# Inverting the chunk matrices of a gated delta-rule scan by 16 by 16 halves, with the joins in the scan's last rounds

## The reference, cut to what matters

```python
tmat = eye + beta[:, None] * (k @ k.T) * dec_strict          # unit lower triangular, per chunk
wk, uv = triangular_solve(tmat, [beta * gam * k, beta * v])
a_qk = (q @ k.T) * dec_incl
def step(s, ...):
    u = uv - wk @ s
    o = gam * (q @ s) + a_qk @ u
    s = g_end * s + k_dec.T @ u
```

## Time and profile before

| | |
|---|---|
| median of 3 runs | 3227.69 us (3227.17 to 3240.73) |
| the profiled execution | 3231.66 us, span 3229.6 us, mean granted TensorE clock 0.917 |
| PE busy | 2796.0 us (87% of the span) |
| DVE, ACT, POOL busy | 1320.1, 1064.8 and 1286.7 us |
| phase of the heads | from about 190 to 1245 us |

### The profile page before, as it was taken

The page is one execution under the profiler, slowest core; times in us unless marked ns, Lnnn a source line. Parts: engine busy times, 40 slices in busy tenths (PEclk is TensorE's granted clock), DMA queues, the critical chain, the costliest instruction groups (busy, mean ns, idle before and its releaser), DMA issues. The chain is left out here.

```text
span 3229.6 us, 45798 instructions
## 1 busy us (share of the span) xinstructions
PE 2796.0 (87%) x17857; PEld 1766.7 (55%) x18113; DVE 1320.1 (41%) x1836; ACT 1064.8 (33%) x1794; POOL 1286.7 (40%) x1450
## 2 busy tenths in 40 slices
PE   5666878878887878989998978999899999999996
PEld 2234656656665665567676754455455555555554
DVE  5233555545555544666767655351311111110112
ACT  4123343443443443244454535211512111101122
POOL 1036747657467450276666531242212111211121
PEclk8777988988889878999999999999999999999997
DMA  7511121112111113223334336241011111111111
GB/s 278 179 57 52 33 74 56 45 59 71 39 66 64 39 52 108 90 67 83 87 85 132 81 91 223 76 165 46 25 41 39 46 39 39 39 46 39 37 35 65
DMA packets 244520, 241.22 MB, mean 75 GB/s; under 512 B 26285, under 2 KB 216286, under 8 KB 241014
## 3 DMA queue, kind: packets, MB, share of 16 engines
q1 hardware_dynamic: 231238, 207.32, 20.9%
q10 hardware_dynamic: 11520, 21.01, 1.7%
q0 software_dynamic: 1584, 10.49, 0.8%
HBM read 191.12 MB, written 43.45 MB: 73 GB/s over the span
## 5 line engine op out<-in xcount | busy, mean ns | idle before, releaser
L171 POOL TENSOR_TENSOR w_pair<-w_raw,w_pair 128x1024 bf16<-128x1024 f32 (+1 forms) x156 | 367.6, 2357 | 1226.7 <-ACT w_pair L166 1225.0
L182 PE MATMUL t_out<-hn,w_pair 128*128 128x512 bf16 (+1 forms) x3102 | 572.2, 345 | 17.1 <-DVE hn L2759 10.5
L1043 PE MATMUL bank<-hn,w_pair 128*128 128x512 bf16 (+1 forms) x2251 | 476.2, 364 | 41.9 <-POOL w_pair L171 22.1
L182 PEld LDWEIGHTS t_out<-hn,w_pair 128*128 128x128 bf16 x3168 | 310.5, 98 | 278.5 <-issue 18.3
L182 PE MATMUL t_out<-ys,w_pair 128*128 128x512 bf16 (+1 forms) x2118 | 397.6, 347 | 10.6 <-PEq L2400 8.4
L1043 PEld LDWEIGHTS bank<-hn,w_pair 128*128 128x128 bf16 x2304 | 239.1, 104 | 227.5 <-issue 50.6
L2095 PE MATMUL s_banks<-hn,w_pair 128*128 128x512 bf16 (+1 forms) x1677 | 315.1, 344 | 7.5 <-PEq L1656 4.9
L182 PEld LDWEIGHTS t_out<-ys,w_pair 128*128 128x128 bf16 x2160 | 213.4, 99 | 190.1 <-issue 16.8
L166 ACT ACTIVATE w_pair<-w_raw 128x1024 bf16<-128x1024 f32 x156 | 164.1, 1054 | 440.4 <-PE t_out L182 321.3
L182 PE MATMUL b_out<-ys,w_pair 128*128 128x512 bf16 (+1 forms) x1129 | 216.6, 353 | 40.6 <-DVE ys L2495 29.5
L2095 PEld LDWEIGHTS s_banks<-hn,w_pair 128*128 128x128 bf16 x1728 | 169.3, 98 | 142.5 <-POOL w_pair L171 5.2
(11 more groups left out here) (402 smaller groups left out, 4412.9 us busy)
## 6 DMA issues: line engine op xcount, KB each, us to landing
w_raw<-in_w_in SPq DMA_DIRECT2D x56, 512.0 KB, 4.0
w_ada_rows<-in_w_ada SPq DMA_DIRECT2D x24, 1024.0 KB, 5.3
w_raw<-in_w_gu SPq DMA_DIRECT2D x44, 512.0 KB, 3.8
hn<-scratch_g SPq DMA_DIRECT2D x24, 640.0 KB, 5.7
scratch_g<-gate_ring ACTq DMA_DIRECT2D x48, 256.0 KB, 2.3
mat<-scratch_cum SPq DMA_DIRECT2D x16, 640.0 KB, 4.7
at<-scratch_cum SPq DMA_DIRECT2D x16, 640.0 KB, 5.7
qg<-scratch_cum SPq DMA_DIRECT2D x16, 640.0 KB, 7.7
```

The costliest lines, as they stand in the source:

```text
L171: pool.tensor_tensor(K.w_pair[:, slot, 1, 0:kt, :], K.w_raw[:, slot, 0:kt, :], K.w_pair[:, slot, 0, 0:kt, :], ALU.subtract).then_inc(K.w_l ...
L182: mm = pe.matmul(out[:, c0:c0 + cn], K.w_pair[:, slot, w, k, :], x[:, a, k, c0:c0 + cn], start=i < 3, stop=i >= 9 * kt - 3)
L1043: mm = pe.matmul(bank[:, 6 + n % 2, 0:cn], K.w_pair[:, slot, w, k, :], K.hn[:, a, k, c0:c0 + cn], start=i == 0, stop=i == 23)
```

## The change

- POOL inverts the 16 by 16 diagonal halves of the 32 by 32 blocks, both at once: 15 steps of a multiply and a subtract, each on 2 times (15 - j) times (j + 1) elements. One more memset clears half of `mat_d`.
- What joins two halves to a block of 32 becomes three parts of 80 matmuls on 32 by 32 tiles of the array, with 16 columns (`join16`). Part W stands in round 6 (rounds count from 0) after its first piece of projection, part Z at the end of round 6, part X after round 7. ACT copies W out (`read_w16`), DVE adds Z and X into `zd` and `ld`.
- DVE's two turns of the inverse move from the tail into round 5 of the scan (places 10 and 11); the adds stand at places 15 and 17.
- The tail is written in another order on PE, DVE, ACT and POOL, and the Q tile comes in nine pieces. The turned values are scaled by DVE (six `tensor_tensor`) and no longer by ACT (twenty `activation`). POOL prepares `mat` before the low half of the V tile. The low half of the Q tile follows that of Z after step 14.

```diff
-                    for j in range(31):
-                        a, b = 31 - j, j + 1
-                        tmp = step[:, 0:a * b].rearrange("p (i c) -> p i c", c=b)
+                    for j in range(15):
+                        a, b = 15 - j, j + 1
+                        tmp = step[:, 0:2 * a * b].rearrange("p (s i c) -> p s i c", s=2, c=b)
                         pool.drain()
-                        pool.tensor_tensor(tmp, mat_in[:, j, j + 1:32].unsqueeze(2).to_broadcast([P, a, b]),
-                                           x[:, j:j + 1, 0:b].to_broadcast([P, a, b]), ALU.mult)
+                        pool.tensor_tensor(tmp, m16[:, :, j, j + 1:16].unsqueeze(3).to_broadcast([P, 2, a, b]),
+                                           x16[:, :, j:j + 1, 0:b].to_broadcast([P, 2, a, b]), ALU.mult)
                         pool.drain()
-                        i = pool.tensor_tensor(x[:, j + 1:32, 0:b], x[:, j + 1:32, 0:b], tmp, ALU.subtract)
+                        i = pool.tensor_tensor(x16[:, :, j + 1:16, 0:b], x16[:, :, j + 1:16, 0:b], tmp, ALU.subtract)
...
+                    if is_head(m):
+                        decays_mat(m)
                     if is_head(n + 1):
                         low(("V", n + 1))
                     if is_head(m):
-                        decays_mat(m)
                         inverse(m, {2: [t for t in (("K", m + 1),) if is_head(t[1])],
-                                    14: [t for t in (("Z", n + 1),) if is_head(t[1])],
-                                    26: [t for t in (("Q", n + 2),) if is_head(t[1])]})
+                                    14: [t for t in (("Z", n + 1), ("Q", n + 2)) if is_head(t[1])]})
...
+                def join16(n, part):
+                    b = bank[:, 2, 0:2 * NB * 16].rearrange("p (i c) -> p i c", c=16)
+                    if part == "W":
+                        pe.wait_ge(s.diag16, 2 * n + 1)
+                    elif part == "Z":
+                        pe.wait_ge(s.diag16, 2 * n + 2)
+                        pe.wait_ge(s.w16, n + 1)
+                    else:
+                        pe.wait_ge(s.z16, n + 1)
+                    for i in range(2 * NB):
+                        d, t = divmod(i, NB)
+                        for q in range(4):
+                            p = slice(32 * q, 32 * q + 32)
+                            if part == "W":
+                                mm = pe.matmul(b[p, i, :], mat[p, d, t, p], zd[p, i, 16:32], start=True, stop=True)
+                            elif part == "Z":
+                                mm = pe.matmul(b[p, i, :], ld[p, i, :], mat_d[p, i, 16:32], start=True, stop=True)
+                            else:
+                                mm = pe.matmul(b[p, i, :], mat_d[p, i, :], ld[p, i, 0:16], start=True, stop=True)
+                    mm.then_inc(s.join16, 1)
...
+                    def join16(place):
+                        if place == 10:
+                            dve.wait_ge(s.inv, n + 1)
+                            dve.transpose(zd[:, :, :].rearrange("p b i -> p i b"), x).then_inc(s.diag16, 1)
+                        if place == 11:
+                            dve.transpose(ld[:, :, :].rearrange("p b c -> p c b"), x.rearrange("p i c -> p c i")).then_inc(s.diag16, 1)
+                        if place == 15:
+                            dve.wait_ge(s.join16, 3 * n + 2)
+                            dve.tensor_tensor(zd[:, 0:2 * NB, 16:32], zd[:, 0:2 * NB, 16:32], b16, ALU.add).then_inc(s.z16, 1)
+                        if place == 17:
+                            dve.wait_ge(s.join16, 3 * n + 3)
+                            dve.tensor_tensor(ld[:, 0:2 * NB, 0:16], ld[:, 0:2 * NB, 0:16], b16, ALU.add)
+                            dve.drain().then_inc(s.diag_out, 1)
...
+                def read_w16(n):
+                    act.wait_ge(s.join16, 3 * n + 1)
+                    act.activation(mat_d[:, 0:2 * NB, 16:32], bank[:, 2, 0:2 * NB * 16].rearrange("p (i c) -> p i c", c=16),
+                                   ACT.Copy, scale=half[:, :]).then_inc(s.w16, 1)
...
+                        for g, (t0, tn) in enumerate(GROUPS):
+                            b = quad(to_read(h, f"VT{g}"), tn)
+                            dve.tensor_tensor(vt[:, 0, t0:t0 + tn, :], b, per_tok(skb[:, t0:t0 + tn], tn), ALU.mult)
+                            dve.tensor_tensor(vt[:, 1, t0:t0 + tn, :], b, per_tok(sk[:, t0:t0 + tn], tn), ALU.mult)
+                            dve.drain().then_inc(s.read_dve, 1)
```

More of the change, by code:

```diff
@@ L794, in read_by_act @@
 def read_by_act(name):
-    return name in ("VT0", "VT1", "VT2") or name[:3] in ("L1V", "L1E", "L2V", "L2F") and name[3] == "1"
+    return name[:3] in ("L1V", "L1E", "L2V", "L2F") and name[3] == "1"
 USES = bank_uses()
@@ L814, in phase_heads @@
         mat = f("mat", 2, NB, C)
-        mat_d, mat_in = f("mat_d", 32, 32), f("mat_in", 32, 32)
+        mat_d, mat_in = f("mat_d", 32, 32), f("mat_in", 33 * 32)
+        half = f("half_col", 1)
         x_step = f("inv_x", 32 * 32 + 256)
@@ L831, in phase_heads @@
         bp, nbg = f("beta_n", 2, 2, NB), f("neg_bg", 2, NB)
-        rk2, sk, skb = f("k_inv2", NB), f("k_len", NB), f("k_len_b", NB)
+        rk2, sk, skb = (mat_in[:, 32 * 32 + 10 * j:32 * 32 + 10 * j + NB] for j in range(3))
         kss, eq = f("k_sum", 2, NB), f("q_eps", 2, NB)
@@ L1189, in _, with piece @@
                     after = [("Q", n + 1)] if is_head(n + 1) else []
-                    def piece(c):
+                    def piece(first, end):
                         if after:
-                            fill(after, 24 * c, 24)
+                            fill(after, first, end - first)
+                    if h == -1:
+                        for last in [x for x in USES if x[0] < h][-3:]:
+                            pe.wait_ge(s.read_act if read_by_act(last[1]) else s.read_dve, READ_NUMBER[last])
+                        for part in "WZX":
+                            join16(n, part)
+                    piece(0, 8)
                     if is_head(n):
-                        for g in range(3):
-                            turned(h, f"KT{g}", lambda t: blk(kt[:, n % 3], t))
                         pe.wait_ge(s.diag_out, n + 1)
@@ L1219, in _ @@
                         sums(h, "SSK", lambda t: rw[:, 2 + off(t):2 + off(t) + C])
+                    piece(14, 20)
+                    if is_head(n):
+                        pe.wait_ge(s.y_diag, 2 * n + 1)
+                        for d in range(2):
+                            for half in range(2):
+                                level2_v(h, d, half)
+                        pe.wait_ge(s.silu, SILU["V", n] + 1)
+                        for g in range(3):
+                            turned(h, f"VT{g}", lambda t: blk(vt_raw, t))
+                    piece(20, 36)
                     if h >= 0:
@@ L1233, in _ @@
                             products(h, f"G{g}", kt[:, m % 3], kt[:, m % 3])
+                    piece(52, 62)
+                    if is_head(n):
+                        for g in range(3):
+                            products(h, f"QK{g}", kt[:, n % 3], qt)
+                    piece(62, 72)
             @block.scalar
@@ L1401, in _ @@
                     if is_head(n):
-                        level2(h, 0)
-                        for d in range(2):
-                            act.wait_ge(s.qg_in[d], 16 * (n + 1))
-                            act.activation(qg[:, d, :], qg[:, d, :], ACT.Exp).then_inc(s.qg_exp, 1)
                         for d in range(2):
@@ L1408, in _ @@
                             act.activation(at[:, d], at[:, d], ACT.Exp).then_inc(s.at_exp, 1)
+                    if is_head(m):
+                        for d in range(2):
+                            act.wait_ge(s.mat_clamp, 2 * m + d + 1)
+                            act.activation(mat[:, d], mat[:, d], ACT.Exp).then_inc(s.mat_exp, 1)
+                    if is_head(n):
+                        level2(h, 1)
                     if h >= 0:
@@ L1418, in _ @@
                     if is_head(m):
-                        for d in range(2):
-                            act.wait_ge(s.mat_clamp, 2 * m + d + 1)
-                            act.activation(mat[:, d], mat[:, d], ACT.Exp).then_inc(s.mat_exp, 1)
                         act.wait_ge(s.mat, m + 1)
@@ L1461, in tap @@
                             conv_tap(t, w)
+                        if h >= 0 and is_head(n):
+                            join16(place)
                     for i, units in enumerate(ROUNDS if h >= 0 else ()):
```

181 lines of the change are left out of this document (100 added, 81 removed).

## The result

The changed kernel takes **3248.02 us** (median of 20 runs, 3234.84 to 3255.18); the kernel before took 3230.86 us beside it (20 runs). The ratio is 1.0048, interval 1.0037 to 1.0058: a little slower, where 2% faster was forecast. The profiled execution took 3241.40 us (span 3239.6).

A forecast was written before the change was run, and what follows sets the result against it. Scans were taken as bound by PE's own work, tails by some 22.5 us of waits and the clock. Six turns (-47), the front (-5) and the last tail (-7.5) gave -60 us: 3168 us, range 3145 to 3190.

The forecast's parts named there:

- The inverse: On POOL, it ends 25 us into the scan; DVE asks about 38 us in; cost nothing, 13 us to spare.
- The joins: On PE, 1.85 us for each part of 160 records; W and Z add 3.7 us to the scan, X lies in the tail.
- Start of the tail: From the scan's last output product to `level1_v`: 4.8 us instead of 13.1, the idle 10.9 us gone.
- Middle and end of the tail: PE's work becomes 45 us, ACT's copy starts at 38; the next scan starts at about 53 instead of 65.65 us.
- Start of the scan: The output's low half comes last on DVE ahead of the first `rhs`: 1 us more.
- The sum: Per turn: tail -12.6, joins +3.7, scan's start +1, together -7.9 us; six turns -47, all -60 us.
- At the front: Ahead of the first scan PE's idle 23.39 us becomes 16.5; with scan 0 and the rest of that tail about -5 us.
- at the end: In the last tail, waits of 6.67 and 2 us give way to 3, and ACT's scaling saves 2: -7.5 us.
- no change: A wait not seen takes the first one's place, in the ACT queue above all: 3228 us, chance 0.05.
- the bank ring: Sign of a wrong forecast: a tail as long as before, with the wait on ACT or in the bank ring.
- The slower rival: Joins halve the clock in the scan's rounds 6 and 7, a part costs 5.2 us: 3287 us, chance 0.04.
- the two rivals on the tail's clock: The clock stays up: 3120 us, chance 0.17; or it falls in the tail's first half: 3203 us, chance 0.13.

The follow-up runs named there:

- c1_together: The changed kernel with ACT's exponentials ahead of the Q tile's second chunk, loads behind `level1_v`, and `mat`'s diagonal blocks copied earlier on ACT: 3173.5 us.
- e1_act_order: The changed kernel with ACT's copy of the Q tile's second chunk moved behind the exponentials and the copies of level 2: 3208.4 us.
- d1: The changed kernel's order with the old inverse (31 steps, DVE's two turns at the start of the tail, no joins): 3279.5 us.
- e2: The changed kernel with the output's low half ahead of the turn of `mat_in` on DVE: 3241.5 us.
- e3: The changed kernel with SP's loads at the start of the tail held until `level1_v` is written: 3216.5 us.
- n2: c1_together with the loads held until `level1_e` is written instead of `level1_v`: 3212.5 us.

## Why the prediction was wrong, step by step

- **The inverse: right.** POOL's first step lies at 604.37 and its last at 625.99, 28 us into the scan (25 forecast), and DVE turns it at 644.06, 46 us into it, without a wait. The two turns take 1.97 and 2.07 us and stall nothing.
- **The joins: the work right, its price wrong.** W and X take 1.53 and 1.49 us (1.85 forecast); 0.85, the estimate by the Trainium skill (TensorE: Matmul & The Clock Gate, on packing small matmuls), was too low. But the sum counted PE's time only. A matmul of 16 columns costs 256 bytes of code, and a dense run of them uses up a packet in 1.2 us. In the kernel before such runs stood behind waits of 10.9 us or between pieces, so no row of mine showed this price, and no gap of that trace ends behind a packet of code; the two rows I took, 11.6 and 32.4 ns a record, came from runs of 60 and 40 matmuls. The doubled parts put a part at some 6 us a turn, the shortened ones at 3.3. The scan's +5.5 us (+4.7 forecast) hides this; the tail shows it.
- **"Start of the tail": wrong.** 4.8 us were forecast from the scan's last output product to `level1_v`. It took 4.2 to 5.2 in four tails and 7.8 to 12.5 in three, with gaps of up to 6.42 us and the low clock behind them; in the four, the gaps lie inside `level1_v` or are small. In c1_together it is 4.2 to 6.7.
- **"Middle and end of the tail": the step that cost most.** I put the copy of the Q tile's second chunk at 38 us and the four exponentials right behind it, and let G run beside them. The copy came at 44.9, and G waits for banks that ACT frees behind the exponentials. The list of ACT stands in the section on the change, with the words that the copies of level 2 follow the exponentials; the sum takes from it only that the exponentials follow the copy, and not that G's banks come free behind the copies of level 2. e1_act_order shows the price: 39.6 us. The joins came to 10 us a turn where the sum had 5.55 (three of 1.85), 31 us more over seven turns. Forecast and result lie 80 us apart; if the two prices add, they are 71 of it, but no run undoes both.
- **"Start of the scan": too small.** 1 us was counted for the output's low half; PE waits 3.0 us for `rhs`, since `mat_d` also stands behind a chunk's copy and the weights' high half on ACT and starts at 726.07, with the scan.
- **The sum.** Six tails gave 30.0 us (-12.6 x 6 = -75.6 forecast), the six scans behind them cost 35.0 (+4.7 x 6 = 28.2). At the front -5 became +5.5, at the end -7.5 became +3.8: there the same gaps (up to 4.81 us) and part X stand in a tail without a Q tile to cover them. That makes 14 us more in the phase; the two spans differ by 10.0 us, the medians by 17.2.
- **The rivals.** The nearest was "no change", a wait in the ACT queue that takes the place of the first one, at 0.05. It gave the time to 0.6%, in part by luck: it names the ACT queue, and neither the code nor the 10 us of the joins. I listed the ACT queue and the bank ring as signs of error, and did not follow the list down to the instruction that frees the bank. The slower rival, a clock halved by the joins in the scan, did not come: the scans ran at 0.97 and 0.93. Of the two rivals on the tail's clock, neither came as described: in the traced tail the clock was low from 684.0 to 687.4, then back at 1.00, and low again from 690.8 to 701.1. But the sum left the clock as it was, and it came out lower: four stretches with 23.0 us of PE's work in the tail and a fifth with 5.9 at the start of the scan, as against 21.75 in four, the last of which reaches into the scan. Over the eight scans and seven tails PE's work at the low clock rose from 163 to 188 us, which would be some 12 us less at the full clock, an estimate from these two sums.

## What to carry to other kernels

Count code beside time: many small matmuls are a load on PE's instruction supply, and a wait that is removed may have been the time in which that supply caught up. When an order is rewritten, follow each list down to the instruction that frees a buffer, not only to the one that makes a value: here the place of one copy in ACT's list was worth 39.6 us, more than twice what the change lost. When a part is put back to see what it was worth, the rest of the order can hold it up, as POOL's list did in d1. And a change that loses may hold a gain: with ACT's order mended and the loads held back the changed kernel is 1.6% faster than the kernel before. How much of that the halves and joins bring stays open.

## What the runs showed of the hardware

- An fp32 matmul of 32 by 32 by 16 took 256 bytes of PE's program; the program came in packets of 16 KB. In a part issued twice PE stopped for 2.36 us with no other transfer under way, and in the change for 6.42 us beside loads that kept 82% of the DMA engines busy. It went on 1.5 and 1.4 us after the packet had landed.
- The stops are places in the program, not in time: 3 records before the end of part X in the third tail, in the change and in e1, e2, e3, c1 and n2 alike.
- Part X on four diagonal tiles took 9.5 ns a record (1.49 us for 157), where the 120 records of `level1_e` took 11.6.
